# High weight halves stored 132 words apart per tile, so that stationary tiles begin at many offsets modulo 512 bytes

## What is computed

```python
for l in range(2):
    h = rmsnorm(x, norm_mix[l])
    q, k, v, u, ug, ga, gb = split(h @ w_in[l])
    a_out = sliding_window_attention(rope(rmsnorm(q)), rope(rmsnorm(k)), v, sinks[l])
    c_out = conformer_conv(u, ug, conv_w[l], ...) @ w_conv_out[l]
    x = x + (sigmoid(ga) * a_out + sigmoid(gb) * c_out) @ w_out[l]
    g, up = split(rmsnorm(x, norm_ffn[l]) @ w_gate_up[l])
    x = x + (silu(g) * up) @ w_down[l]
```

```python
h = _rmsnorm(x, g_pre_mix)
q, k, v, g, u, sv, a_ret, a_sgu = split(h @ w_in)
y_ret = (layernorm(retention(q, k, v)) * silu(g)) @ w_ret_o
y_sgu = (gelu(u) * spatial(layernorm(gelu(sv)))) @ w_sgu_o
x = x + _rmsnorm((sigmoid(a_ret) * y_ret + sigmoid(a_sgu) * y_sgu) @ w_out, g_post_mix)
a, b = split(conv3(_rmsnorm(x, g_pre_ffn) @ w_up))
x = x + _rmsnorm((gelu(a) * b) @ w_down, g_post_ffn)
```

## Time and profile before

| | |
|---|---|
| median of 2 runs | 2197.57 us (2197.36 to 2197.77) |
| profiled execution, first to last instruction | 2195.6 us |
| around it (median minus span) | 2.0 us |
| TensorE matmuls | 10528, busy 2182.7 us (99%) |
| VectorE | 1378.5 us (63%) |
| ScalarE | 965.5 us (44%) |
| GpSimd | 74.7 us (3%) |
| DMA | 208.39 MB, mean 95 GB/s |
| granted TensorE clock, mean | 0.999 of full speed |

### The profile page before, as it was taken

The page is one execution under the profiler, slowest core; times in us unless marked ns, Lnnn a source line. Parts: engine busy times, 40 slices in busy tenths (PEclk is TensorE's granted clock), DMA queues, the critical chain, the costliest instruction groups (busy, mean ns, idle before and its releaser), DMA issues.

```text
span 2195.6 us, 28930 instructions
## 1 busy us (share of the span) xinstructions
PE 2182.7 (99%) x10528; PEld 1813.8 (83%) x10528; DVE 1378.5 (63%) x1978; ACT 965.5 (44%) x1392; POOL 74.7 (3%) x103
## 2 busy tenths in 40 slices
PE   9999999999999999999999999999999999999998
PEld 6878888888888878888888888888888899888887
DVE  7999954444345999954444334654776568888723
ACT  5678544443223588544443223331554344333412
POOL 0000020000010000020000010000000000000000
PEclk9999999999999999999999999999999999999999
DMA  5221222222223211222222224223222231222222
GB/s 182 75 78 65 96 96 96 96 96 84 93 93 123 90 62 64 94 96 100 99 99 92 80 92 156 97 77 131 84 91 87 96 135 39 100 101 97 94 96 77
DMA packets 35397, 208.39 MB, mean 95 GB/s; under 512 B 4512, under 2 KB 5024, under 8 KB 14816
## 3 DMA queue, kind: packets, MB, share of 16 engines
q1 hardware_dynamic: 35296, 207.07, 27.0%
HBM read 201.15 MB, written 2.10 MB: 93 GB/s over the span
## 4 chain that ended last, share of the span: by engine, by line
PE 94%; ACT 3%; DVE 2%; issue 1%; DMA 0%; SPq 0%; DVEq 0%
PE mm L1794 25%; PE mm L1796 25%; PE mm L1795 25%; PE sp L1794 4%; PE sp L1795 4%; PE sp L1796 4%; PE sp L1896 1%; PE ob L1924 1%; DVE conv_y L1171 1%; ACT probs L584 1%; DVE probs L1201 1%; ACT probs L592 1%; PE sp L1911 0%; DMA x<-in_x_dram 0%; PE ob L1796 0%
## 5 line engine op out<-in xcount | busy, mean ns | idle before, releaser
L1794 PE MATMUL mm<-in_hi,w_hi 128*128 128x512 f32 (+1 forms) x1696 | 663.8, 391 | 3.8 <-DVE in_lo L1104 2.1
L1796 PE MATMUL mm<-in_hi,w_lo 128*128 128x512 f32 (+1 forms) x1696 | 657.0, 387 | 0.0
L1795 PE MATMUL mm<-in_lo,w_hi 128*128 128x512 f32 (+1 forms) x1696 | 657.0, 387 | 0.0
L525 ACT ACTIVATE w_hi<-w_raw 128x2048 fp32r<-128x2048 f32 (+3 forms) x193 | 346.2, 1794 | 674.8 <-PE mm L1796 557.9
L1070 DVE TENSOR_TENSOR w_lo<-w_raw,w_hi 128x2048 fp32r<-128x2048 f32 (+3 forms) x193 | 422.3, 2189 | 239.5 <-ACT w_hi L525 239.0
L1794 PEld LDWEIGHTS mm<-in_hi,w_hi 128*128 128x128 f32 x1696 | 318.5, 188 | 75.1 <-DVE in_lo L1104 6.0
L1796 PEld LDWEIGHTS mm<-in_hi,w_lo 128*128 128x128 f32 x1696 | 318.4, 188 | 65.8
L1795 PEld LDWEIGHTS mm<-in_lo,w_hi 128*128 128x128 f32 x1696 | 318.6, 188 | 64.1 <-issue 1.0
L1171 DVE SCALAR_TENSOR_TENSOR conv_y<-conv_in,parl,conv_y 128x512 f32<-128x512 f32 x240 | 170.0, 747 | 1.7
L1081 DVE TENSOR_TENSOR tB<-mm,rstd 128x512 f32<-128x512 f32 x54 | 37.3, 691 | 172.8 <-PE mm L1796 172.8
L1794 PE MATMUL mm<-act_hi,w_hi 128*128 128x512 f32 x352 | 136.9, 389 | 0.0
(11 more groups left out here) (429 smaller groups left out, 3257.0 us busy)
## 6 DMA issues: line engine op xcount, KB each, us to landing
w_raw<-in_w_dram SPq DMA_DIRECT2D x160, 1024.0 KB, 4.8
w_raw<-in_w_dram SPq DMA_DIRECT2D x32, 704.0 KB, 3.9
w_raw<-in_w_dram SPq DMA_DIRECT2D x5, 512.0 KB, 4.7
out_dram<-z_rows SPq DMA_DIRECT2D x8, 256.0 KB, 2.1
rope<-in_rope_dram SPq DMA_DIRECT2D x3, 512.0 KB, 3.6
x<-in_x_dram SPq DMA_DIRECT2D x4, 256.0 KB, 4.9
x<-in_x_dram SPq DMA_DIRECT2D x2, 512.0 KB, 7.9
sq<-ssum SPq DMA_DIRECT2D x32, 32.0 KB, 1.8
```

Of the source, the lines that this page charges most:

```text
L525: e.activation(whi[:, slot, 0:cols], raw[:, slot, 0:cols], ACT.Copy).then_inc(s_whi, whi_out.up())
L1794: MM(out, ah, bh, start=first, stop=False, **kw)
L1795: MM(out, ah, bl, start=False, stop=False, **kw)
L1796: return MM(out, al, bh, start=False, stop=last, **kw)
```

## The change

`w_hi` gets a step of 132 words (528 bytes) from tile to tile in place of 128, so that its 32 tiles begin 16 bytes further each, modulo 512; each tile itself stays contiguous. It grows by 512 bytes. `w_lo` has the shape of tiles too, but stays dense. The padding `to_512_bytes` is left out, which takes 384 bytes away with its rounding. All activations thus begin 128 bytes further, at 256 modulo 512, while `w_lo`, `ones` and `sum_hi` stay at 128.

Distances after the change, weights stationary: -128 (that is 384) for every tile of `w_lo`, and 16j - 128 for tile j (0 to 31, over both slots) of `w_hi`, which takes each multiple of 16 once. With the weights moving, they are the same with the other sign, and a moving 512 columns of `w_hi` consist of four pieces of 128 with 16 bytes between them. `w_out` and retention's own operands keep a distance of 0 from the activations. `sum_lo` still begins at 160.

No engine has another instruction, another order or another wait: the lists of both programs are the same, but for the shape that ScalarE and VectorE write `w_hi` and `w_lo` in (128x16x128 in place of 128x2048).

```diff
+WSTEP = P + 4
...
-        whi = sb("w_hi", [P, 2, CH], F32R)
-        wlo = sb("w_lo", [P, 2, CH], F32R)
+        whi = sb("w_hi", [P, 2, CH // P, WSTEP], F32R)
+        wlo = sb("w_lo", [P, 2, CH // P, P], F32R)
...
-        sb("to_512_bytes", [P, 92])
...
+        def w_cols(t, slot, a, b):
+            return t[:, slot, a // P:b // P, 0:P]
+        def w_tile(t, slot, k):
+            return t[:, slot, k, 0:P]
+        def raw_cols(slot, a, b):
+            return raw[:, slot, a:b].rearrange("p (k c) -> p k c", c=P)
...
-                e.activation(whi[:, slot, 0:cols], raw[:, slot, 0:cols], ACT.Copy).then_inc(s_whi, whi_out.up())
+                e.activation(w_cols(whi, slot, 0, cols), raw_cols(slot, 0, cols), ACT.Copy).then_inc(s_whi, whi_out.up())
...
-                TT(wlo[:, slot, first:cols], raw[:, slot, first:cols], r32(whi[:, slot, first:cols]),
+                TT(w_cols(wlo, slot, first, cols), raw_cols(slot, first, cols), r32(w_cols(whi, slot, first, cols)),
                    ALU.subtract).then_inc(s_w, w_out.up())
...
-                    a = slice((at + j) * P, (at + j + 1) * P)
-                    ins = mm3(four[bank], whi[:, slot, a], wlo[:, slot, a], hi_[:, k, :], lo_[:, k, :],
+                    ins = mm3(four[bank], w_tile(whi, slot, at + j), w_tile(wlo, slot, at + j), hi_[:, k, :], lo_[:, k, :],
                               first and j == 0, last and j == len(ks) - 1)
...
-                    ws = slice(T * j, T * j + T)
-                    ins = mm3(four[wide_banks[b]], xh[:, k, ts], xl[:, k, ts], whi[:, slot, ws], wlo[:, slot, ws],
+                    ws = (slot, T * j, T * j + T)
+                    ins = mm3(four[wide_banks[b]], xh[:, k, ts], xl[:, k, ts], w_cols(whi, *ws), w_cols(wlo, *ws),
                               k == 0, k == KT - 1)
```

More of the change, by code:

```diff
@@ L533, in prep_part @@
             def prep_part(cs):
-                e.activation(whi[:, 0, cs], raw[:, 0, cs], ACT.Copy).then_inc(s_whi, whi_out.up())
+                e.activation(w_cols(whi, 0, cs.start, cs.stop), raw_cols(0, cs.start, cs.stop), ACT.Copy).then_inc(s_whi, whi_out.up())
             def prep_rest():
@@ L1115, in prep_and_sum @@
                 for cs in (slice(0, CH // 2), slice(CH // 2, CH)):
-                    TT(wlo[:, 1, cs], raw[:, 1, cs], r32(whi[:, 1, cs]), ALU.subtract).then_inc(s_w, w_out.up())
+                    TT(w_cols(wlo, 1, cs.start, cs.stop), raw_cols(1, cs.start, cs.stop),
+                       r32(w_cols(whi, 1, cs.start, cs.stop)), ALU.subtract).then_inc(s_w, w_out.up())
                     if cs.start == 0:
@@ L1136, in _ @@
             first_lo((2,))
-            more = slice(CH // 4, CH // 2)
             e.wait_ge(s_whi, whi_in.next())
-            TT(wlo[:, 0, more], raw[:, 0, more], r32(whi[:, 0, more]), ALU.subtract).then_inc(s_do, own.up())
+            TT(w_cols(wlo, 0, CH // 4, CH // 2), raw_cols(0, CH // 4, CH // 2), r32(w_cols(whi, 0, CH // 4, CH // 2)),
+               ALU.subtract).then_inc(s_do, own.up())
             first_lo((3,))
@@ L2011, in token_major @@
                         e.wait_ge(ready.sem, ready.next())
-                    ws = slice(256 * k, 256 * k + 256)
-                    ins = mm3(mm[bank][:, 0:256], xh[:, k, ts], xl[:, k, ts], whi[:, slot, ws], wlo[:, slot, ws],
+                    ws = (slot, 256 * k, 256 * k + 256)
+                    ins = mm3(mm[bank][:, 0:256], xh[:, k, ts], xl[:, k, ts], w_cols(whi, *ws), w_cols(wlo, *ws),
                               k == 0, k == KT - 1)
@@ L2122, in half_product @@
                         e.wait_ge(ready.sem, ready.next())
-                    a = slice(at + k * P, at + (k + 1) * P)
-                    ins = mm3(out, wh[:, a], wl[:, a], xh[:, k, hs], xl[:, k, hs], k == 0, k == KT - 1)
+                    ins = mm3(out, wh[:, at + k, 0:P], wl[:, at + k, 0:P], xh[:, k, hs], xl[:, k, hs], k == 0, k == KT - 1)
                 return ins
@@ L2136, in out_half @@
             def out_half(m, hs, ks=range(KT), ready=None):
-                return half_product(four[m % 4][:, 0:TH], wo[:, m // 2, 0, :], wo[:, m // 2, 1, :],
-                                    CH // 2 * (m % 2), hs, ready, ks)
+                wh, wl = (wo[:, m // 2, i, :].rearrange("p (k c) -> p k c", c=P) for i in range(2))
+                return half_product(four[m % 4][:, 0:TH], wh, wl, KT * (m % 2), hs, ready, ks)
             def up_half(j, hs, ks=range(KT), ready=None):
-                return half_product(four[j][:, hs], whi[:, j // 2, :], wlo[:, j // 2, :],
-                                    CH // 2 * (j % 2), hs, ready, ks)
+                return half_product(four[j][:, hs], whi[:, j // 2, :, :], wlo[:, j // 2, :, :],
+                                    KT * (j % 2), hs, ready, ks)
             e.wait_ge(s_w, w_in.next())
@@ L2192, in _ @@
                         e.wait_ge(s_mmf, taken.next())
-                        half_product(bank, whi[:, c, :], wlo[:, c, :], CH // 2 * d,
+                        half_product(bank, whi[:, c, :, :], wlo[:, c, :, :], KT * d,
                                      slice(0, T)).then_inc(s_mm, tiles.up())
@@ L2210, in rows_product @@
                     k = 2 * c + j
-                    ws = slice(j * D + d * T, j * D + d * T + T)
+                    ws = (c % 2, j * D + d * T, j * D + d * T + T)
                     ts = slice(b * P, (b + 1) * P)
@@ L2216, in rows_product @@
                         e.wait_ge(s_xe, 2 * b + d + 1)
-                    ins = mm3(rows[b][d], acth[:, k, ts], actl[:, k, ts], whi[:, c % 2, ws], wlo[:, c % 2, ws],
+                    ins = mm3(rows[b][d], acth[:, k, ts], actl[:, k, ts], w_cols(whi, *ws), w_cols(wlo, *ws),
                               k == 0, k == FT - 1)
```

## The result

The changed kernel takes 2234.82 us (2234.65 to 2235.0, 2 runs) against 2197.57: the ratio is 1.017, with a 95% interval of 1.014 to 1.0199. It is slower by 37 us, of the sign and kind that was forecast, 13 us under the forecast's own time and 2 us under the forecast's own range of 2237 to 2276 us.

What follows compares the result with a forecast made beforehand. TensorE, busy 99% of the span, was taken to be bound by matmul pitch alone; 6.3 ns x 8000 = 50 us, other terms 0, on a 2195.6 us span plus 2.0 us around it gave 2248 us, range 2194 to 2285.

Steps and rivals of the forecast that it cites:

- The locked step: 512-column matmuls on TensorE: with equal distances they settle at 226.7 ns each; another distance throws them out for some ten matmuls.
- Its last sentence: The prediction's closing doubt: it fails above all if alternating distances have a locked step of their own.
- 6.3 ns for 8000 matmuls: 512-column matmuls on w_hi and w_lo: 233 ns unlocked against 226.7, 50 us in all, ends 42 and 66 us.
- The mean of ten: Ten matmuls behind a single disturbance at a sum: 232.0 ns each, the lower end for an unlocked matmul.
- the first four pitches: First four matmuls behind a sum, where the disturbance is fresh: 235 ns mean, upper end of the plain case.
- Terms at nothing: Parts of the change taken at 0: 256-column matmuls, ScalarE's and VectorE's 16 pieces, transfers, moved tensors.
- 256 columns: 576 of the 960 matmuls of 256 columns use w_hi and w_lo: -0.6 us at most, taken at 0.
- the bank change, not the distance, disturbs: Rival at the sums: slow pitches come from another PSUM bank; 2198 us; no lock lost or half of it: 0.21.
- The rule of two independent read ports: SBUF reads: a load takes no bandwidth from the running matmul, so 2198 us; no lock lost or half: 0.21.
- The variant with a period shorter than 512 bytes: Readers count distance modulo something shorter, 64 say; half of the 50 us comes, 2223 us; within the 0.21.
- the spread takes the interference away: Rival: 16-byte steps take most loads out of collision; 94 us off, 2104 us, with half 2151; in part or whole 0.16.
- each load costs 9.3 ns: Rival, always freshly disturbed: every load at another distance costs what -32 did, 78 us, 2276 us, up to 2310; 0.08.

Runs made afterwards that it cites:

- a_pad_out: The kernel before without the padding to_512_bytes, both weight halves dense: every load on w_hi, w_lo and w_out at -128 bytes; 2241.74 us, ratio 1.0203.
- f_sums: The kernel before with parl and pars moved behind the squares, so the sums' operands begin at 128 modulo 512 like everything else; 2197.21 us, ratio 1.0.
- c_lo128: The kernel before with w_lo alone 128 bytes further on, everything behind it in place modulo 512; 2230.52 us, ratio 1.0152.
- b_32: The kernel before with 100 words of padding in place of 92, one distance of -32 bytes throughout; 2246.51 us, ratio 1.0224.
- i_minus64: The kernel before with 108 words of padding in place of 92, one distance of -64 bytes throughout; 2214.37 us, ratio 1.0077.
- h_off16: The kernel before with both weight halves beginning 16 bytes later, distances 16 and 272; 2234.25 us, ratio 1.0168.
- d_lo256: The kernel before with w_lo alone 256 bytes further on, distances 0, 0, +256; 2197.39 us, ratio 1.0001.
- k_minus16: The kernel before with both weight halves in one tensor, 240 bytes later, a distance of -16 modulo 256 throughout; 2209.37 us, ratio 1.0052.

## Why the prediction came out right, and where it was wrong

**What bounds the kernel.** Right: the cost is in the pitch alone, 1730 matmuls for 1768 in the window, with no wait and no other engine in it.

**The locked step.** Here the reasoning was half wrong. "When every matmul has the same distance, they fall into a step in which a matmul costs 226.7 ns": that holds for 0 and 256. Eight kernels with another distance throughout (in two of them counted modulo 256) took 2209 to 2255 us. At -128, -64, -32, +4, +64 and +96 not one run of twelve pitches of 226 or 227 ns is found on the weights; at +16 and -16 the step exists, in 24% and 30% of the pitches, and TensorE doesn't come back to it reliably once it is out. What the trace before showed was that a single load at -32 disturbs ten matmuls at 0; that it was the change of distance and not the distance itself had no row, and I took it for granted. The forecast survived since the changed kernel has both, and that is luck: by the prediction's own reasoning a_pad_out would have been as fast as the kernel before, and it is slower than the changed one. Its last sentence asked for the wrong doubt: not an even step under alternating distances, but none under equal ones. The right reading of the earlier trace rows is: out of step, it takes some ten matmuls **at 0** to find the step; at six of the eight other distances no such step was ever found, and at +16 and -16 it can stay lost.

**The size.** 6.3 ns for 8000 matmuls was the term that was mis-sized. The mean pitch is 231.7, not 233: 4.8 ns over the mean before, for 8400; the sums above give 41 us in place of 50. The mean of ten, 232.0, was nearly exact, and the shift of 1 ns towards the first four pitches was not called for. That ten matmuls recovering at a distance of 0 should have the mean of a kernel full of other distances had no reason behind it; the eleven kernels that have loads off 0 and 256 on the weights have means of 228.6 to 234.1 ns. Besides, gaps and plain float32 gave back 2.6 us. Half of it, 1.3 us, is the shorter wait for attention's `probs`, which are there when TensorE arrives later; I had that slack at nothing. So the pitch lies inside the forecast's 231.5 to 236 ns, and the time 2 us under its 2237. 50 us forecast, 37 measured.

**Terms at nothing.** 256 columns: -0.9 us, 0.3 beyond the end that was named. ScalarE and VectorE: 1 us of work in all, none on the path, and 0.3 us in the wait for `w_lo`.

**The rivals.** That the bank change, not the distance, disturbs, is refuted by f_sums. The rule of two independent read ports (the Trainium skill, TensorE: Matmul & The Clock Gate, "What happens when you issue a matmul") doesn't hold here as far as it says that a load takes nothing from the matmul that runs: moving the activations alone by 128 bytes (a_pad_out) costs 44 us. The variant with a period shorter than 512 bytes was right in kind: the period is 256 and no divisor of it, since by any of them 128 would be the same as 0, and a_pad_out is slow. It halved nothing, though, since a neighbour of a load off its place pays as well (c_lo128). That the spread takes the interference away was wrong: no distance has a mean below 226.7 ns, and none came near 215.8, the estimate by the formula that the Trainium skill gives on the same page, section "Back-to-back issue gap". That each load costs 9.3 ns was wrong as well; b_32, made of such loads alone, has 6.4 on the mean before.

**What stays open.** Why TensorE finds an even step at 0 and 256 each time, at +16 and -16 at times and at the others that ran never; why -64 is cheap and +64 is not, while -32 and +32 are alike; what 4 and 16 bytes cost by the distance and what by the tile's own place; and what the 13 ns are that a matmul costs over its columns at the best distance. Whether a better distance than 0 exists wasn't settled: of 32 multiples of 8 bytes (modulo 256) all occurred mixed, but only eight as a kernel's single distance (0 among them), and +4 besides. No version was found that beats the kernel before. The 384 matmuls of 256 columns with moving weights, put at +64 while all others stay at 0, would be worth 384 x 6.4 ns = 2.5 us by i_minus64, an estimate that no run tests.

## What to carry to other kernels

In a kernel that keeps TensorE full with float32r matmuls of 512 columns, each with a load of its own, lay out the tensors so that the stationary tile begins at a multiple of 256 bytes from the moving tile that is read while it is loaded, and look at this first when a size in the list of tensors changes: a padding of 8 words more cost 2.2% of the whole (b_32). The test is quick: pitches from the starts of matmuls, which should be even; where they wander over 224 to 241 ns, count the distance. A kernel's mean can hide two paces, so look at stretches, too (h_off16). And one disturbance seen in a trace shows that a thing matters, not which regime it leads to: ask for a run in which it is constant before you say that variation is the cause.

## What the runs showed of the hardware that was not expected

- A distance of 256 bytes is as good as 0 (d_lo256: ratio 1.0001), and the changed kernel's pitches repeat themselves after 256 bytes. The sign counts at 64 (+64: 1.0213, -64: 1.0077), not at 32 (233.3 ns both ways). Weights moved by a single word give a ratio of 1.0217 (g_off4), whether by the distance or by their own place.
- The same distance can have two paces that last: at +16 an even 226.7 ns over 351 matmuls and 233.2 ns elsewhere in one kernel (h_off16), at -16 226.7 and 228.4 ns (k_minus16).
- Matmuls of 256 columns with moving weights take 113.5 ns at +64 and 119.9 at 0.
- Off 0 the pitches go in cycles: at +64 234, 233, 233 (and 236, 231, 235, 231 at 1950 us of the same kernel); at -64 232, 226, 229; at -16, where uneven, 229, 230, 229, 226; at -128 a peak of 241 comes with every seventh matmul.
- A load off its place costs its neighbour as well: means of 232.4, 234.0 and 226.9 ns in c_lo128, where only the first of the three has such a load.
- Writing 16 pieces of 128 words 528 bytes apart costs ScalarE and VectorE nothing against one of 2048: 1795 for 1794 ns and 2189 for 2189 (the kernel before is on the page with these).
